# Router products by token, affinities moved on chip, and an earlier first gather in a hybrid encoder layer with experts

## The reference

```python
x = x + ga1 * rms_norm(merged @ w_out, g_post1)
h2 = rms_norm(x, g_pre2) * (1.0 + sc2) + sh2
# expert_choice_ffn(h2, ...), for prompt and sample apart:
aff = jax.nn.softmax((t @ w_router).astype(jnp.float32), axis=-1)
gate, idx = lax.top_k(aff.T, cap)
xe = t[idx]
a = jnp.einsum('ecd,edf->ecf', xe, w_gate)
u = jnp.einsum('ecd,edf->ecf', xe, w_up)
ye = jnp.einsum('ecf,efd->ecd', jax.nn.silu(a) * u, w_down)
ye = ye * gate[..., None].astype(ye.dtype)
out = jnp.zeros_like(t).at[idx.reshape(-1)].add(ye.reshape(-1, d))
x = x + ga2 * rms_norm(out, g_post2)
```

## Time and profile before

| | us |
|---|---|
| median of three runs | 2862.66 |
| lowest and highest | 2862.07, 2864.35 |
| profiled execution, its own time | 2865.04 |
| span of its trace | 2863.2 |
| PE busy in the span | 2664.6 (93%) |
| DVE busy | 1783.7 (62%) |
| ACT busy | 1332.5 (47%) |
| POOL busy | 300.0 (10%) |

### The profile page before, as it was taken

One profiled execution on the slowest core, in us unless ns is written; L12 is line 12 of the kernel. 1 busy time (PEld: TensorE's weight loads), 2 busy tenths in 40 slices (PEclk: granted clock), 3 DMA queues, 4 the chain that ended last, 5 costly groups with the idle time before them and its releaser, 6 DMA issues. The chain is left out here.

```text
span 2863.2 us, 48388 instructions
## 1 busy us (share of the span) xinstructions
PE 2664.6 (93%) x20566; PEld 2134.3 (75%) x20566; DVE 1783.7 (62%) x2147; ACT 1332.5 (47%) x1409; POOL 300.0 (10%) x244
## 2 busy tenths in 40 slices
PE   4799999999999988993999999999999999999993
PEld 2688888888888877871777777777777777777772
DVE  2575775757511044547777777777777777776775
ACT  3543534435311121441555555555555555555552
POOL 2010010100000012111011011110111111110110
PEclk9999999999999999995999999999999999999996
DMA  9201101110142154326788888888888888788886
GB/s 346 78 20 43 45 24 53 31 50 24 40 173 83 68 195 158 121 103 242 251 289 299 285 299 294 288 283 286 298 287 294 295 298 286 275 299 289 282 293 229
DMA packets 285640, 564.97 MB, mean 197 GB/s; under 512 B 24545, under 2 KB 90945, under 8 KB 285169
## 3 DMA queue, kind: packets, MB, share of 16 engines
q1 hardware_dynamic: 277744, 540.90, 52.9%
q0 software_dynamic: 7680, 20.98, 3.1%
HBM read 514.52 MB, written 47.28 MB: 196 GB/s over the span
## 5 line engine op out<-in xcount | busy, mean ns | idle before, releaser
L2182 DVE TENSOR_TENSOR we_low<-ring,we_high 128x2048 fp32r<-128x2048 f32 x384 | 878.0, 2291 | 365.8 <-ACT we_high L2131 364.9
L2131 ACT ACTIVATE we_high<-ring 128x2048 fp32r<-128x2048 f32 x384 | 735.8, 1917 | 442.0 <-PE ps_ey L2103 281.9
L1268 PE MATMUL ps_a<-h_high,w_high 128*128 128x512 f32 (+1 forms) x696 | 252.4, 363 | 8.9 <-DVEq L980 8.9
L1269 PE MATMUL ps_a<-h_low,w_high 128*128 128x512 f32 (+1 forms) x696 | 247.6, 356 | 0.0
L1270 PE MATMUL ps_a<-h_high,w_low 128*128 128x512 f32 (+1 forms) x696 | 247.3, 355 | 0.0
L2070 PE MATMUL ps_ep<-ring,xp 128*32 128x256 f32 x4096 | 234.3, 380 | 0.0
L2101 PE MATMUL ps_ey<-we_high,hidT_high 128*128 128x512 f32 x512 | 206.6, 404 | 0.0
L2045 PE MATMUL ps_eg<-we_high,xs_high 128*128 128x512 f32 x512 | 206.2, 403 | 0.3 <-DVE xs_low L2206 0.3
L2070 PEld LDWEIGHTS ps_ep<-ring,xp 128*32 128x32 f32 x4096 | 126.5, 110 | 99.5 <-issue 22.5
L2048 PE MATMUL ps_eu<-we_low,xs_high 128*128 128x512 f32 x512 | 200.1, 391 | 0.0
L2047 PE MATMUL ps_eu<-we_high,xs_high 128*128 128x512 f32 x512 | 200.1, 391 | 0.0
(11 more groups left out here) (293 smaller groups left out, 4974.9 us busy)
## 6 DMA issues: line engine op xcount, KB each, us to landing
ring<-in_w_gate SPq DMA_DIRECT2D x256, 512.0 KB, 9.1
ring<-in_w_up SPq DMA_DIRECT2D x256, 512.0 KB, 10.5
ring<-in_w_down SPq DMA_DIRECT2D x256, 512.0 KB, 4.3
w_raw<-in_w_in SPq DMA_DIRECT2D x52, 512.0 KB, 3.8
w_ring<-in_w_ada SPq DMA_DIRECT2D x20, 1024.0 KB, 11.9
sig_dram<-sig SPq DMA_DIRECT2D x15, 640.0 KB, 5.4
sig_g<-sig_dram SPq DMA_DIRECT2D x16, 512.0 KB, 3.9
yT_dram<-pair SPq DMA_DIRECT2D x8, 640.0 KB, 5.3
```

Source lines behind the costliest of these rows:

```text
L1268: pe.matmul(out, w_high, x_high, start=start, stop=False)
L1269: pe.matmul(out, w_high, x_low, start=False, stop=False)
L2131: act.activation(w_high[:, s % SPLIT], t.ring[:, s % RAW], ACT.Copy).then_inc(s_high, 1)
L2182: dve.tensor_tensor(w_low[:, s % SPLIT], t.ring[:, s % RAW], w_high[:, s % SPLIT], ALU.subtract).then_inc(s_low, 1)
```

## The change

It has five parts.

1. `route` swaps its operands: the turned tokens are loaded and the router weights stream past, so the logits of a tile come out as tokens by experts, all ten tiles in one bank `ps_l`. The copies to `lgT` and the ten transposes back are gone; the maximum waits for the last product.
2. `affT` goes by three transfers from its place in on-chip memory to the 48 rows of a tile `t.shared`, which lives through both phases, at the end of `phase_residual`. The store to `aff_dram` and the three loads of `phase_choice` are gone.
3. The residual sum of the last tile (tile 9) is done by VectorE behind `scaled(9)` and no longer by GpSimd.
4. The first expert's gather is issued by GpSimd inside `phase_choice`: the prompt rows after `idx_p`, the sample rows after `idx_s`. The row tiles move out of `phase_experts`.
5. In `phase_experts`, `gate_up(b, 0)` and `gate_up(b, 1)` wait for the first half of the split rows only and `gate_up(b, 2)` for the second. On TensorE `turn_x(0, 2)` moves behind `gate_up(0, 1)`.

A scratch tile `m12` of an earlier phase shares `t.shared`. The diff, cut to its core:

```diff
@@ phase_residual
-            for tl in range(NT):
+            for tl in range(NT - 1):
                 pool.wait_ge(s["scaled"], tl + 1)
                 pool.tensor_tensor(x1[:, tl % 3], x1[:, tl % 3], x[:, tl % 3], ALU.add).then_inc(s["x1"], 1)
...
-                    mm = pe.matmul(ps_l[tl % 2][0:NE, 0:P], w_r[:, c], h2T[:, tl % 2, c], start=(c == 0), stop=(c == KC - 1))
+                    mm = pe.matmul(ps_l[:, tl * NE:(tl + 1) * NE], h2T[:, tl % 2, c], w_r[:, c], start=(c == 0), stop=(c == KC - 1))
...
-            pe.wait_ge(s["lc"], NT)
-            for tl in range(NT):
-                mm = pe.transpose(ps_l[0][:, tl * NE:(tl + 1) * NE], lgT[:, tl * P:(tl + 1) * P], t.ident[0:NE, 0:NE])
-            mm.then_inc(s["lt"], 1)
...
+                if tl == NT - 1:
+                    dve.wait_ge(s_x[tl % 3], 16 * (tl // 3 + 1))
+                    dve.wait_ge(s["x1"], tl)
+                    dve.tensor_tensor(x1[:, tl % 3], x1[:, tl % 3], x[:, tl % 3], ALU.add).then_inc(s["x1"], 1)
...
-            sp.dma_start(t.aff_dram, affT[:]).then_inc(s["st"], 16)
-            sp.wait_ge(s["st"], 32)
+            for r, (o, m) in enumerate(((SEQS[0], HALF), (SEQS[0] + HALF, HALF), (0, SEQS[0]))):
+                sp.dma_start(t.shared[r * NE:(r + 1) * NE, 0:m], affT[:, o:o + m]).then_inc(s["st"], 16)
+            sp.wait_ge(s["st"], 64)
@@ phase_choice
-        aff = sb("aff", [R, HALF])
+        aff = t.shared[0:R, 0:HALF]
...
-            for h in range(2):
-                o = SEQS[0] + h * HALF
-                sp.dma_start(aff[h * NE:(h + 1) * NE], t.aff_dram[:, o:o + HALF]).then_inc(s_a, 16)
-            sp.dma_start(aff[2 * NE:R, 0:SEQS[0]], t.aff_dram[:, 0:SEQS[0]]).then_inc(s_a, 16)
...
+            for k, (rows, idx) in enumerate(((t.rows_p, t.idx_p), (t.rows_s, t.idx_s))):
+                pool.wait_ge(s_idx, k + 1)
+                pool.tensor_tensor(tick[:, 1:2], tick[:, 0:1], tick[:, 0:1], ALU.add)
+                pool.drain()
+                pool.indirect_dma_start(out=rows[:], out_offset=None, in_=t.xn_dram,
+                                        in_offset=bass.IndirectOffsetOnAxis(ap=idx[:, 0:1], axis=0)).then_inc(t.s_gather, 16)
...
-            dve.tensor_copy(t.idx_p[:], cols[0:CP, 1, 2 * NE:R])
+            dve.tensor_copy(t.idx_p[:], cols[0:CP, 1, 2 * NE:R]).then_inc(s_idx, 1)
...
-            dve.tensor_scalar(t.idx_s[:], place[:], float(SEQS[0] + HALF), None, ALU.add)
+            dve.tensor_scalar(t.idx_s[:], place[:], float(SEQS[0] + HALF), None, ALU.add).then_inc(s_idx, 1)
@@ phase_experts
-            gather(0)
             gather(1)
...
-                if i == 0:
-                    pe.wait_ge(s_xl, 2 * (e + 1))
-                    if b >= 1:
-                        pe.wait_ge(s_hid, b)
+                if i % 2 == 0:
+                    pe.wait_ge(s_xl, 2 * e + i // 2 + 1)
+                if i == 0 and b >= 1:
+                    pe.wait_ge(s_hid, b)
...
-            for r in range(3):
-                turn_x(0, r)
+            turn_x(0, 0)
+            turn_x(0, 1)
             for b in range(NBLK + 1):
                 if b < NBLK:
                     gate_up(b, 0)
                     gate_up(b, 1)
+                if b == 0:
+                    turn_x(0, 2)
```

More of the change, by code:

```diff
@@ L406, in phase_heads @@
         qk = sb("qk", [P, 2, 2, P])
-        m12 = sb("m12", [P, 2, 256])
+        m12 = t.shared[:].rearrange("p (k x) -> p k x", k=2)
         rqkT = sb("rqkT", [P, 2, NTOK])
@@ L1502, in phase_residual @@
         std = sb("std_r", [P, 2, NT])
-        lgT = sb("lgT", [NE, NTOK])
         affT = sb("affT", [NE, NTOK])
+        HALF = SEQS[1] // 2
         lg = sb("lg", [P, NT, NE])
@@ L1508, in phase_residual @@
         ps_t = [psum(f"ps_rt{i}") for i in range(2)]
-        ps_l = [psum(f"ps_l{i}") for i in range(2)]
+        ps_l = psum("ps_l")
         names = ("cut", "mhigh", "mlow", "o", "ss", "var", "std", "scaled", "x1", "ss2", "var2", "std2", "n", "t", "ta", "tv", "l",
-                 "lc", "lt", "sm", "exp", "aff", "at", "junk", "zero", "st", "ofree", "done", "wohigh", "wolow")
+                 "sm", "exp", "aff", "at", "junk", "zero", "st", "ofree", "done", "wohigh", "wolow")
         s = {n: sem(n) for n in names}
@@ L1721, in _ @@
             split(1)
-            for k in range(NT + 3):
+            for k in range(NT + 2):
                 if k < NT:
@@ L1731, in _ @@
                     modulate(k - 2)
-                if k >= 3:
-                    logits(k - 3)
-            dve.wait_ge(s["lt"], 1)
-            lp = ps_l[0][:, 0:NT * NE].rearrange("p (t e) -> p t e", e=NE)
+            dve.wait_ge(s["l"], NT)
+            lp = ps_l[:, 0:NT * NE].rearrange("p (t e) -> p t e", e=NE)
             dve.tensor_reduce(mx[:], lp, AX_X, ALU.max)
@@ L1814, in phase_choice @@
         w_ada = t.w_ada[0][:, 5 * D:6 * D].rearrange("(p i k) n -> i p k n", i=PER, k=2)
-        s_a, s_flip, s_f, s_t, s_cols, s_b = (sem(n) for n in ("a", "flip", "f", "t", "cols", "b"))
+        s_flip, s_f, s_t, s_cols, s_b = (sem(n) for n in ("flip", "f", "t", "cols", "b"))
+        s_idx = sem("idx")
+        tick = sb("tick_c", [1, 2])
         block = ctx.enter_context(nc.Block())
@@ L1852, in _ @@
             pool.memset(post[:], 0.0)
+            pool.memset(tick[:], 0.0)
             pool.drain()
@@ L1867, in _ @@
             dve.drain()
-            dve.wait_ge(s_a, 48)
             for k in range(0, CS, 8):
                 v = best[:, k:k + 8]
-                dve.max(out=v, in_=aff[:])
+                dve.max(out=v, in_=aff)
                 dve.drain()
-                dve.max_index(out=found[:, k:k + 8], in_max=v, in_values=aff[:])
-                dve.match_replace(out=aff[:], in_to_replace=v, in_values=aff[:], imm_value=-1.0)
+                dve.max_index(out=found[:, k:k + 8], in_max=v, in_values=aff)
+                dve.match_replace(out=aff, in_to_replace=v, in_values=aff, imm_value=-1.0)
                 dve.drain()
@@ L1935, in phase_experts @@
         w_high, w_low = (sb(n, [P, SPLIT, 2048], F32R) for n in ("we_high", "we_low"))
-        rows_s, rows_p = sb("rows_s", [CS, D]), sb("rows_p", [CP, D])
+        rows_s, rows_p = t.rows_s, t.rows_p
         xs = sb("xs", [P, 4, CS])
@@ L1952, in phase_experts @@
         s_ht, s_hth, s_htl, s_htp = sem("ht"), sem("hth"), sem("htl"), sem("htp")
-        s_rows, s_xt, s_xev, s_xh, s_xl = sem("rows"), sem("xt"), sem("xev"), sem("xh"), sem("xl")
+        s_xt, s_xev, s_xh, s_xl = sem("xt"), sem("xev"), sem("xh"), sem("xl")
         s_oact, s_odve, s_oprompt = sem("oact"), sem("odve"), sem("oprompt")
@@ L1992, in gather @@
                     pool.indirect_dma_start(out=rows[:], out_offset=None, in_=t.xn_dram,
-                                            in_offset=bass.IndirectOffsetOnAxis(ap=idx[:, e:e + 1], axis=0)).then_inc(s_rows, 16)
+                                            in_offset=bass.IndirectOffsetOnAxis(ap=idx[:, e:e + 1], axis=0)).then_inc(t.s_gather, 16)
             pool.memset(tick[:], 0.0)
             pool.drain()
-            gather(0)
             gather(1)
@@ L2020, in turn_x @@
                 if r == 0:
-                    pe.wait_ge(s_rows, 32 * (e + 1))
+                    pe.wait_ge(t.s_gather, 32 * (e + 1))
                 if n >= 1:
@@ L2336, in build_program @@
     t.moe_dram = scratch("moe_dram", (NTOK, D))
-    t.aff_dram = scratch("aff_dram", (NE, NTOK))
     t.w_gate_v, t.w_up_v = (w[0].rearrange("e (c p) (b f) -> e b p c f", p=P, f=512) for w in (t.w_gate, t.w_up))
@@ L2345, in build_program @@
         t.head_cols = sb("head_cols", [P, HEADS, 4])
+        t.shared = sb("shared", [P, 512])
         t.c_silu = sb("c_silu", [P, KC, 2])
@@ L2400, in build_program @@
         t.idx_s, t.idx_p, t.idx_q = sb("idx_s", [CAPS[1], NE], U32), sb("idx_p", [CAPS[0], NE], U32), sb("idx_q", [P, NE], U32)
+        t.rows_s, t.rows_p = sb("rows_s", [CAPS[1], D]), sb("rows_p", [CAPS[0], D])
+        t.s_gather = ctx.enter_context(nc.semaphore("gather"))
         phase_choice(nc, t)
```

5 lines of the change are left out of this document (removed).

## The result

The changed kernel takes 2872.99 us, the median of seven runs (2872.19 to 2875.66), beside 2863.41 for the kernel before in the same rounds (seven runs, 2862.07 to 2864.97): 1.0034 of it, 95% interval 1.0025 to 1.0044. That is slower by more than the 0.2% that counts as a difference here, and above the range of the prediction, which ended at 2872. The profiled execution took 2875.66 us, with a span of 2873.9; it is the slowest of the seven, 2.7 above their median.

The account below looks back on a forecast made before the run. PE was taken as the bound, without slack from the first prompt products on. Terms +0.1, -0.9, +0.4, +1.3 and +1.6 sum to +2.5 us: 2865.2 against the median (2867.5 on the profiled execution); range 2859 to 2872.

Parts of the forecast that it names:

- the router's +0.1: Router tail: last sum on VectorE delays turn(8) by 1.2 us, cut copy and transposes save 1.1; net +0.1.
- the gather's +0.4: Choice-to-experts block change: waiting for GpSimd's gather costs 2.4 us, but x_rows(0, 0) starts only 0.4 later.
- the half rows with the clock in their hole, +2.9: First expert products: earlier start followed by a 3.7 us PE hole, +1.3; low clock behind it, +1.6.
- the hand-over: Affinities kept on chip between router and choice: first maximum of the choice 0.9 us earlier, bounds 0.6 to 1.2.
- rival B: Router tail: clock stays low through turn(9), route(8), route(9) and the transposes; +4.7 us on the forecast, 2869.9; chance 0.33.
- a longer issue of the gather: Gather in the choice: an issue of 2.73 us instead of 1.19 would make its term +2.0.
- Rival C: Block change does not wait for the gather (-1.7 us) and clock holds in PE's hole: 2861.5; chance 0.11.
- the forecast: Main case: all five terms together cost +2.5 us, own range 2862 to 2868.5; chance 0.46.
- rival D: Route: 128-column loads do not speed up with the clock, 2.1 us more on each of eight tiles, about 2882; chance 0.05.
- Rival E: Route: the swapped record takes half the old one's time, 8 us saved, 2857; chance 0.05.
- X + 2.9: Expert start: PE's first product comes 2.9 us after X, the start of x_rows(0, 0), instead of 5.85.
- The bound: Clock behind PE's hole before gate_up(0, 2): costs 2.9 us if low for 6 us, 1.6 expected.

Follow-up runs that it names:

- a_old_sum: The changed kernel with part 3 undone, so GpSimd adds the last tile again: 2874.23 us, 1.0038 of the kernel before.
- c_after: The changed kernel run once more, unaltered: 2874.20 us, 1.0036 of the kernel before.
- c_wide_pass: The changed kernel with seven of eight route products streaming 128 columns instead of 16, so other tokens are chosen: 2868.90 us, 1.0018 of the kernel before.
- c_hybrid: d_best with swapped 16-column operands for route tiles 0 to 6, old operands for the last three: 2861.43 us, 0.9989 of the kernel before.
- e_room: d_best with the router weights' tile 448 bytes longer, the added part unread: 2865.46 us, 1.0006 of the kernel before.
- e_padded: d_best with swapped operands streaming 128 columns, router weights in a tile behind all others: 2860.99 us, 0.9990 of the kernel before.
- d_padded: d_best with swapped operands streaming 128 columns, the weights' tile grown by 448 bytes, shifting tiles behind it: 2863.51 us, 0.9999 of the kernel before.
- e_after_padded: The changed kernel with 128 columns streaming in route from a weights tile of their own, reference outputs kept: 2868.97 us, 1.0019 of the kernel before.
- b_marker: The changed kernel with both first-expert gathers in the expert block and a drain and memset behind the first: 2871.57 us, one run.
- d_best: The changed kernel with parts 1 and 3 undone, only prompt rows gathered in the choice, x_rows(0, 2) behind low(3): 2862.01 us, 0.9993 of before.

## Why the prediction was wrong

The stages came in the order in which they were worked out, and each term has its sign. Three terms failed: the router's +0.1 measured +4.46 with the transposes behind the softmax, the gather's +0.4 measured +3.45, and the half rows with the clock in their hole, +2.9, measured +4.41. That is 8.9 us too little; the loop (-1.41), the hand-over (0.5 less gain) and the rounds (-0.39) make it the 7.6 us by which the sum missed. The first two failed in the mechanism, the third in the size. The range held rival B and a longer issue of the gather; it did not hold the landing, and B together with that lies outside.

**Part 4, the end of the block.** "Now the block can end only when GpSimd is through, about 1339.0" put the end at the issue of the gather, +2.4 us. Up to the issue's end the working held: 2.15 us behind `idx_s` for 2.32. But the block ends at the landing: +5.61. The delay in front of X, given as +0.4 with bounds to +2.0, was 5.61 - 2.16 = +3.45. The number was in the traces of before: rows issued by GpSimd had let PE start at 1343.93, long after their issue. The sentence "then it drains" passed over it. Rival C, that the block change would not wait for the gather, was wrong in the other direction.

**Part 1, rival B instead of the forecast.** The step that failed is the router's +0.1: it leaves turn(9), route(8), route(9) and the transposes at the times that they had at the full clock, so it takes the clock to come back under route(7) as it did before. The record was equal to the old one at either clock, as it was taken to be, but the clock stayed at 0.50. The price of B, "turn(9), route(8) and route(9) cost 0.85 + 1.4 + 1.4 more, and the ten transposes behind the softmax about 1.0 more", was nearly right: +3.79 in the tail and +0.67 up to the last copy of `affT`, of which 0.1 is the forecast's. Its chance was set at 0.33 with "PE has no gap in the stretch" against it; the window from 1280.0 to 1288.5, 8.46 of 8.50 us busy at 0.50, shows that a PE without a gap is no evidence for the full clock here. The record was right (1.86 for 16), and so rival D falls. By the prediction's estimate from the Trainium skill, TensorE: Matmul & The Clock Gate, section LDWEIGHTS, a tile would be 1.5 us longer if the load of 128 columns were not hidden. The trace does not show that: the tiles in the second half of the loop are 13.61 us apart in place of 13.83. Rival E, that the swap pays, has this much in it: 0.2 us a tile, 1.4 in the loop, unless the clock falls there.

**Part 3.** Right: `variance(1, 8)` is 1.2 us later and `a_old_sum` gives back 1.19. The copies and transposes that were cut gave the 1.1 that was worked out: the maximum follows the last product at once. But with the clock low, what part 3 delays is not made up.

**Part 5.** The hole came where it was put, 3.3 us for 3.7, ended by `low(2)`, and the first expert product at X + 2.89 for X + 2.9. The clock behind it was the mis-sized term: the 3.4 us of low clock taken from the pause of before became 6.1, so hole and clock together cost 4.4 in place of 2.9 (3.1 in `c_after`). The bound, "2.9 if it stays low for 6 us", nearly held: 1.3 + 2.9 is 4.2.

**Part 2.** Right in kind, half in size: -0.43 for -0.9, an issue at 0.63 in place of 0.41.

The -0.39 in the rounds and the merge was not foreseen. It goes with part 3 in every run: 41.05 to 41.10 us with it, 41.4 without. In the traces without part 3 it is one pause of VectorE between two instructions of the rounds, 0.29 to 0.43 us, in which it waits for nothing that the profile shows; with part 3 that pause is not there. Why stays open. Open too is why the transposes behind the softmax run at the low clock in `c_wide_pass`, `c_hybrid`, `e_room` and `e_padded`, where the clock had come back ahead of the maximum, and at the full one in the kernel before, `d_padded` and `e_after_padded`.

## What to carry to other kernels

A transfer that an engine issues just before a phase ends belongs to the end of that phase, with its whole flight: look at when its data land, not at when the issue leaves the list, and issue in the earlier phase only what lands before the barrier's other work is done. A swap of the operands of small products is not settled by the time of one record; look at the granted clock in the stretches behind it, and if it is lost, try the same load with more columns streaming, which cost 0.1 us a tile here. Where a wait is split so that an engine may start earlier, put the lists of the engines that feed it in the new order of need in the same edit.

## What the runs showed of the hardware

- GpSimd's drain waits for its indirect transfers to land: it took 4.71 us behind a gather whose issue took 1.00 us and whose rows landed 4.4 us after the issue began, and in `b_marker` the next instruction ran 0.15 us behind the landing.
- The granted clock can stay low while PE's row is full: 0.50 in a window with 8.46 us busy of 8.50, under float32 products with a 128x128 load and 16 streaming columns. With 128 streaming columns and the same loads it rose to 1.00. It can also fall while the row is full: in the loop five of the ten traces with 16 columns there show one stretch of low clock, of about 3.4 us, that begins right behind route(0); none of the ten others does. In `c_after` PE's last pause, 0.43 us, ended 2.9 us before the fall (timeline, then windows, PE):

```profile
1182.46 1.06 PE L1580 MATMUL ps_rt<-ident,yT 128*128 128x128 f32 x8 [0.43 <-ACT h2T L1634]
```

```profile
1176.00:1184.80 8.80, 8.37 (x49) 1.00 0.36 91
1184.80:1188.60 3.80, 3.80 (x13) 0.58 0.50 203
```

- A float32 load of 128x128 with 16 columns streaming takes 0.12 us a record at the full clock (1.86 for 16) and 0.21 at the low one (3.43 for 16); with 128 columns streaming it takes the same 0.12.
- Tiles in on-chip memory that start 448 bytes further on made products of 128x512 2% longer by their records (403 and 398 ns in `e_room` for 395 and 390 in `d_best`) and 3% by their starts (11.1 us a tile for 10.8), with nothing else changed.
